# 64-dimension attention heads taken in pairs, one head on each half of TensorE's array

## The chip, the cores and the metric

One core of one Trainium2 chip runs the whole program. The metric is the device time of one execution in microseconds (us). The kernel before took 1958.06 us, the median of 3 runs (1953.44 to 1959.31).

The engines are named as in the profile: PE is TensorE's matmul side and PEld its weight loads, DVE is VectorE, ACT is ScalarE, POOL is GpSimd, SP is SyncE, which here only issues DMAs. SBUF is the on-chip memory, PSUM the eight accumulator banks that PE writes (128 partitions, 512 float32 columns in each bank).

## The reference, cut to what matters

Two two-layer models run one after the other over 256 tokens of width 1024, in float32. Four places in them are attention. Two have heads of 64 output dimensions:

```python
# layer 0 of the first model: 8 neighbourhood heads and 8 latent (MLA) heads
sc = einsum('bchd,bicjhd->bhcij', q_row, k_win) * 64 ** -0.5 + bias
p = softmax(sc);  out = einsum('bhcij,bicjhd->bchd', p, v_win)
# ...
q = concat([q_nope (64), rope(q_pe) (32)]);  k = concat([k_nope, k_pe])   # 96 wide
sc = einsum('bqhd,bkhd->bhqk', q, k) * 96 ** -0.5
p = softmax(sc);  out = einsum('bhqk,bkhd->bqhd', p, v)                   # v is 64 wide
# layer 1 of the first model: 16 dilated heads, 3 window groups each
sc = where(valid, einsum('bqhd,bqjhd->bhqj', q_blk[gi], k_sel[gi]) * 64 ** -0.5, NEG_INF)
outs, lses = softmax-weighted values and log-sum-exp of each group
out = sum(softmax(lses) * outs)
```

The other two (memory attention and forgetting attention in the second model) have heads of 128 dimensions. Around them stand norms and the large projections and MLPs, which make up most of the work.

## The kernel before, in words

The program is a list of stages made by `make_plan`; each engine walks the same list, and semaphores tie the engines together. Nothing is scheduled automatically: the order on each engine is the order in which the code is written. Between attention stages PE multiplies weight chunks that SP has loaded, ACT has rounded (`W_hi`, L914) and DVE has split (`W_lo`, L1127).

An attention stage (`kind == "attend"`) has a list of heads. The stage named "even" has 8 neighbourhood heads followed by 8 latent heads; "dilated" has 16 heads with three key groups; "memory0" has 4 and "fox" 12 heads of 128 dimensions. For each head n the engines do this:

- PE `scores(n)` (L680): queries times keys for two blocks of 128 queries. The stationary operand has 64 partitions for a neighbourhood or dilated head (partitions 0 to 63 for an even head, 64 to 127 for an odd one, `pb`), 96 for a latent head. One call in the code is two recorded matmuls, because the operands are plain float32. A neighbourhood or latent head has 4 recorded matmuls of 256 columns; a dilated head has 4 of 256 and 8 of 128.
- DVE `soft(n)`: scale and bias into SBUF (L1166 dilated, L1174 neighbourhood), then the row maximum (L1199). A latent head has only the maximum, read from PSUM (L1161, L1162).
- ACT `exps(n)` (L983): two exponentials with their row sums.
- DVE `normalise(n)`: reciprocal (L1204) and two multiplications (L1207).
- PE `transposes(n)` (L698): 4 transposes of the 128x128 blocks of probabilities, 8 for a dilated head.
- ACT `keep_pt(n)` (L993): the transposed probabilities from PSUM to SBUF, one copy of 512 columns, two for a dilated head.
- PE `values(n)` (L712, for the other two groups of a dilated head L719): values (stationary, 64 columns wide) times probabilities. The output lands on PSUM partitions 0 to 63 or 64 to 127 of bank 2 or 3.
- DVE `output(n)` (L1218): that result to SBUF.

PE's order per head is `transposes(n)`, `scores(n+3)`, `values(n)`. DVE's is `normalise(n+1)`, `output(n-1)`, `soft(n+3)`; ACT's is `keep_pt(n)`, `exps(n+2)`. The first heads' scores are issued inside the last projection of the stage before (`open_attention`): 3 heads for "even", 2 for "dilated". DVE runs their `soft` there too, ahead of the copy that ends the projection (L1345, L1364). Two heads before the end ACT also stages the input of the projection that follows (`stage_early`, L976), whose first matmul is L600.

## Time and profile before

| | |
|---|---|
| span of the profiled execution | 1952.7 us |
| its whole time | not recorded apart from the span; the 3 timed runs took 1953.44, 1958.06 and 1959.31 us |
| PE busy | 1882.7 us (96%) |
| DVE, ACT, POOL busy | 1219.9, 933.9, 273.2 us (62%, 48%, 14%) |
| mean granted TensorE clock | 0.992 |
| "even" attention, first transpose to the matmul behind it | 86.55 to 128.28 us |
| "dilated" attention, the same | 571.90 to 644.98 us |
| DMA busy share in the middle of both | 0.00 to 0.01 |

The page says that PE carries most of the chain that ended last. The two stages touched by the change are 42 and 73 us of the 1953. In a timeline row the first number is the start, the second the time from the first start to the last end of the merged instructions, so rows of pipelined matmuls overlap a little; in the chain the pieces add up.

### The profile page before, as it was taken

Reading aid. Unit: us, or ns where it says so; the run is one execution under the profiler, and the core shown is the slowest. Engines: PE = TensorE matmul, PEld = TensorE weight load, DVE = VectorE, ACT = ScalarE, POOL = GpSimd, SP = SyncE. Lnnn points to the kernel's source line nnn. Section 1 sums busy time; section 2 is a strip of 40 time slices with the busy share of each in tenths; the row PEclk is TensorE's granted clock in tenths of the full one; section 3 lists DMA queues with packets and bytes.
Section 4 is the critical chain, followed back from the end, with each engine's and each line's share of the span. In section 5 each row is a group of like instructions: output and inputs, shape, how many; then the busy total and the mean of one; then the engine's idle time right before and its main releaser. Section 6 shows DMA issues by size and latency. Waiting matters only on the chain.

```text
span 1952.7 us, 27728 instructions
## 1 busy us (share of the span) xinstructions
PE 1882.7 (96%) x9804; PEld 1580.0 (81%) x9804; DVE 1219.9 (62%) x1452; ACT 933.9 (48%) x1384; POOL 273.2 (14%) x219
## 2 busy tenths in 40 slices
PE   8899999999999999999999999999999999989998
PEld 6668887777778788888888878888888888778886
DVE  6866645766778566465656656664646656756654
ACT  5354444334345544454445445454544545545453
POOL 2110012211200101220011750002000011020012
PEclk9899999999999999999999999999999999999999
DMA  5415555454430465545555535555535555345553
GB/s 189 172 49 167 174 195 190 154 176 166 156 125 1 126 187 192 192 160 191 190 183 183 193 131 179 186 178 196 186 110 192 193 175 191 108 140 162 182 191 131
DMA packets 214812, 319.32 MB, mean 164 GB/s; under 512 B 5984, under 2 KB 167008, under 8 KB 214496
## 3 DMA queue, kind: packets, MB, share of 16 engines
q1 hardware_dynamic: 213616, 313.45, 48.6%
q0 software_dynamic: 848, 4.85, 0.6%
q8 instruction: 37, 0.61, 0.1%
q10 hardware_dynamic: 288, 0.23, 0.0%
q14 instruction: 23, 0.19, 0.0%
HBM read 317.46 MB, written 1.05 MB: 163 GB/s over the span
## 4 chain that ended last, share of the span: by engine, by line
PE 87%; DVE 9%; ACT 2%; issue 2%; POOL 1%; DMA 0%; DVEq 0%; ACTq 0%; POOLq 0%
PE PS L595 24%; PE PS L600 12%; PE PS L602 12%; PE PS L601 12%; PE PS L593 12%; DVE W_lo L1127 4%; PE PS L589 4%; PE PS L680 3%; PE PS L712 2%; PE PS L590 2%; PE PS L698 1%; PE PS L665 1%; PE PS L719 1%; DVE U L1374 1%; DVE U L1375 0%
## 5 line engine op out<-in xcount | busy, mean ns | idle before, releaser
L1127 DVE TENSOR_TENSOR W_lo<-W_raw,W_hi 128x1024 fp32r<-128x1024 f32 x598 | 772.7, 1333 | 290.7 <-ACT W_hi L914 289.4
L595 PE MATMUL PS<-XN,W_hi 128*128 128x512 f32 x2072 | 739.3, 396 | 0.0
L914 ACT ACTIVATE W_hi<-W_raw 128x1024 fp32r<-128x1024 f32 x598 | 598.3, 1050 | 183.0 <-PE PS L602 172.0
L593 PE MATMUL PS<-XN,W_lo 128*128 128x256 f32 x2072 | 578.9, 279 | 0.0
L595 PEld LDWEIGHTS PS<-XN,W_hi 128*128 128x128 f32 x2072 | 389.2, 188 | 79.9
L593 PEld LDWEIGHTS PS<-XN,W_lo 128*128 128x128 f32 x2072 | 391.1, 189 | 13.9
L1536 POOL TENSOR_TENSOR SX<-U,SX 128x512 fp32r<-128x512 f32 (+1 forms) x98 | 128.8, 1319 | 1352.2 <-ACT SX L976 1352.2
L600 PE MATMUL PS<-W_hi,SX 128*128 128x512 f32 x780 | 303.9, 390 | 1.4 <-issue 1.3
L601 PE MATMUL PS<-W_lo,SX 128*128 128x512 f32 x780 | 303.1, 389 | 0.0
L602 PE MATMUL PS<-W_hi,SX 128*128 128x512 f32 x780 | 303.0, 389 | 0.0
L927 ACT ACTIVATE T<-PS 128x512 f32<-128x512 f32 x152 | 91.0, 599 | 437.7 <-PE PS L595 437.7
L1138 DVE TENSOR_TENSOR T<-PS,T 128x512 f32<-128x512 f32 x128 | 88.5, 691 | 244.1 <-ACT T L927 244.1
L600 PEld LDWEIGHTS PS<-W_hi,SX 128*128 128x128 f32 x780 | 146.4, 188 | 32.4 <-issue 2.5
L602 PEld LDWEIGHTS PS<-W_hi,SX 128*128 128x128 f32 x780 | 146.4, 188 | 30.5
L976 ACT ACTIVATE SX<-U 128x512 fp32r (+2 forms) x98 | 60.6, 629 | 230.5 <-PE PS L602 230.5
L601 PEld LDWEIGHTS PS<-W_lo,SX 128*128 128x128 f32 x780 | 146.4, 188 | 30.1
L600 PE MATMUL PS<-W_hi,XN 128*128 128x512 f32 (+2 forms) x368 | 144.3, 392 | 15.0 <-DVE W_lo L1127 13.2
L601 PE MATMUL PS<-W_lo,XN 128*128 128x512 f32 (+2 forms) x368 | 141.7, 385 | 0.0
L602 PE MATMUL PS<-W_hi,XN 128*128 128x512 f32 (+2 forms) x368 | 141.6, 385 | 0.0
L589 PE MATMUL PS<-XN,W_hi 128*128 128x512 f32 x296 | 119.0, 402 | 8.6 <-DVE W_lo L1127 7.6
L600 PEld LDWEIGHTS PS<-W_hi,XN 128*128 128x128 f32 x368 | 70.2, 191 | 33.4 <-DVE W_lo L1127 19.6
L590 PE MATMUL PS<-XN,W_lo 128*128 128x256 f32 x296 | 82.4, 278 | 0.0
(145 smaller groups left out, 1599.3 us busy)
## 6 DMA issues: line engine op xcount, KB each, us to landing
W_raw<-in_ffn_w_gate_up SPq DMA_DIRECT2D x88, 1024.0 KB, 5.1
W_raw<-in_mlp_w SPq DMA_DIRECT2D x64, 1024.0 KB, 5.2
W_raw<-in_ffn_w_down SPq DMA_DIRECT2D x44, 1024.0 KB, 4.9
W_raw<-in_od_w_in SPq DMA_DIRECT2D x36, 1024.0 KB, 5.2
W_raw<-in_a_w_in SPq DMA_DIRECT2D x14, 1024.0 KB, 5.0
W_raw<-in_mem_w_kv SPq DMA_DIRECT2D x8, 1024.0 KB, 5.3
W_raw<-in_w_kvf SPq DMA_DIRECT2D x8, 1024.0 KB, 5.4
W_raw<-in_ev_w_in SPq DMA_DIRECT2D x6, 1024.0 KB, 5.3
```

The lines of the kernel that those rows point to most:

```text
L589: mm(bank, wT(W_hi, slot, k, fb), both, start=True, stop=False)
L590: mm(bank[:, S:], wT(W_lo, slot, k, fb), xn[:, k, 0, :], start=False, stop=False)
L593: mm(bank[:, S:], wT(W_lo, slot, k, fb), xn[:, k, 0, :], start=False, stop=False)
L595: last = mm(bank, wT(W_hi, slot, k, fb), both, start=False, stop=k == KD - 1)
L600: mm(bank, xh, wh, start=start, stop=False)
L601: mm(bank, xh, wl, start=False, stop=False)
L602: return mm(bank, xl, wh, start=False, stop=stop)
L914: A(W_hi[:, slot, halves(h)], W_raw[:, slot, halves(h)], ACT.Copy).then_inc(w_hi, 1)
L927: A(T0[:, pair, :].rearrange("p (f t) -> p f t", f=2), PS[:, 2 * pair:2 * pair + 2, S:2 * S], ACT.Copy).then_inc(cross_out, 1)
L1127: V.tensor_tensor(W_lo[:, slot, halves(h)], W_raw[:, slot, halves(h)], W_hi[:, slot, halves(h)], ALU.subtract).then_inc(w_lo, 1)
L1138: return V.tensor_tensor(dst.rearrange("p (f t) -> p f t", f=2), PS[:, 2 * pair:2 * pair + 2, 0:S], T0[:, pair, :].rearrange("p (f t) -> p ...
L1536: nc.gpsimd.tensor_tensor(SX[:, slot, 1, 0:st["ks"] * S], down_src(st, j), SX[:, slot, 0, 0:st["ks"] * S], ALU.subtract).then_inc(st_lo, 1)
```

## The change

In the stages "even" and "dilated" heads are taken in units of two (an even head and the odd head after it); in "memory0" and "fox" a unit is one head, and the order there stays as it was.

- `scores(u)` issues the two heads' calls alternately. For neighbourhood and dilated heads one is on array rows 0 to 63, the other on rows 64 to 127, each with its own PSUM banks. Latent heads have 96 rows each.
- `values(u)` issues the two heads' calls alternately, one on columns 0 to 63 and one on columns 64 to 127, into the two partition halves of one bank, and counts once on its semaphore.
- `output(u)` copies both halves with one instruction of 128 partitions.
- Transposes, exponentials, maxima and normalisations keep their number and size, but stand in twos.
- The look-ahead is in units. "Even": scores and `soft` lead by 2 units, with 2 units' scores issued in the opening. "Dilated": by 1 unit, with single-buffered score banks; probabilities alternate between two places, the transposed ones have one place.

The line numbers of the new kernel differ: L680 became L707, L698 L725, L712 L742, L719 L751; on DVE L1166 became L1211, L1199 L1244, L1204 L1249, L1207 L1252, L1218 L1264; on ACT L983 became L1022, L993 L1032.

```diff
-                 sm=18752, pt=19776, mem=20800, kpe=22848)
+                 sm=18752, pt=20800, mem=20800, kpe=22848)
...
+                st["paired"] = st["name"] in ("even", "dilated")
+                st["size"] = 2 if st["paired"] else 1
+                st["u0"] = len(units)
+                st["units"] = range(len(units), len(units) + len(st["what"]) // st["size"])
+                units += [range(len(heads) + i, len(heads) + i + st["size"])
+                          for i in range(0, len(st["what"]), st["size"])]
...
-            e["score_banks"] = (4 + n % 2 * 2, 5 + n % 2 * 2) if e["G"] == 3 else (4 + n % 3,)
+            u, i = e["unit"], e["slot"]
+            e["score_banks"] = ((4 + 2 * i, 5 + 2 * i) if e["G"] == 3 else
+                                (4 + 2 * (u % 2) + i,) if e["paired"] else (4 + n % 3,))
...
+            if e["G"] == 3:
+                e["probs"] = region(at + i * width, width) if u % 2 == 0 else T[:, i * width:(i + 1) * width]
+                e["ptile"] = [region(e["R"]["pt"] + (2 * i + g) * 512, 512) for g in range(2)]
+                e["pt_free"] = u
+            elif e["paired"]:
+                e["probs"] = region(at + (2 * (u % 2) + i) * width, width)
+                e["ptile"] = [region(e["R"]["pt"] + (2 * (u % 2) + i) * 512, 512)]
+                e["pt_free"] = u - 1
+            else:
+                e["probs"] = region(at + (n % 3) * width, width) if n % 3 < 2 else T1
+                e["ptile"] = [region(e["R"]["pt"] + (n % 2) * 512, 512)]
+                e["pt_free"] = u - 1
+
+            back = n - 2 * 2 if e["paired"] else n - 3
+            e["probs_back"] = back if back >= 0 and heads[back]["paired"] == e["paired"] else None
...
-        opened = lambda st: 3 if st["name"] in ("even", "fox") else 2
+        opened = lambda st: {"even": 2, "dilated": 1, "memory0": 2, "fox": 3}[st["name"]]
...
-            def scores(n):
-                e = heads[n]
-                for prev in e["score_prev"]:
-                    if heads[prev]["bias"]:
-                        pe.wait_ge(s_read, heads[prev]["read"] + 1)
-                    else:
-                        pe.wait_ge(s_exp, 2 * prev + 2)
+            def scores(u):
+
+                both = [heads[n] for n in units[u]]
+                for e in both:
+                    for prev in e["score_prev"]:
+                        if heads[prev]["bias"]:
+                            pe.wait_ge(s_read, heads[prev]["read"] + 1)
+                        else:
+                            pe.wait_ge(s_exp, 2 * prev + 2)
                 for t in range(TT):
-                    for g in range(e["G"]):
-                        at = e["cols"][t].start + (S + (g - 1) * P if g else 0)
-                        keys = (slice(t * P, (t + 1) * P) if g else
-                                slice(0, min(S, e["cols"][t].stop - at)))
-                        last = mm(e["scores"][:, at:at + keys.stop - keys.start],
-                                  e["q"][g][:, t * P:(t + 1) * P], e["k"][g][:, keys],
-                                  start=True, stop=True)
+                    for g in range(both[0]["G"]):
+                        for e in both:
+                            at = e["cols"][t].start + (S + (g - 1) * P if g else 0)
+                            keys = (slice(t * P, (t + 1) * P) if g else
+                                    slice(0, min(S, e["cols"][t].stop - at)))
+                            last = mm(e["scores"][:, at:at + keys.stop - keys.start],
+                                      e["q"][g][:, t * P:(t + 1) * P], e["k"][g][:, keys],
+                                      start=True, stop=True)
                 last.then_inc(s_score, 1)
...
-            def values(n):
-                e = heads[n]
-                if n >= 2:
-                    pe.wait_ge(h_done, e_out_done(n - 2))
-                d = 64 if e["pb"] or e["bias"] in ("na", "dil") or e["scale"] == 96 ** -0.5 else P
-                o = PS[e["pb"]:e["pb"] + d, 2 + n % 2, 0:S]
-                pe.wait_ge(s_pte, e["group0"] + 1)
+            def values(u):
+
+                both = [heads[n] for n in units[u]]
+                if u >= 2:
+                    pe.wait_ge(h_done, e_out_done(units[u - 2][-1]))
+                for e in both:
+                    d = (64 if e["paired"] else P)
+                    e["o"] = PS[e["pb"]:e["pb"] + d, 2 + u % 2, 0:S]
+                pe.wait_ge(s_pte, both[-1]["group0"] + 1)
                 for kt in range(TT):
-                    skip = P if kt and e["bias"] == "fox" else 0
-                    last = mm(o[:, skip:], e["v"](0, kt), e["ptile"][0][:, kt * S + skip:(kt + 1) * S],
-                              start=kt == 0, stop=kt == TT - 1 and e["parts"] == 1)
-                if e["parts"] == 2:
-                    pe.wait_ge(s_pte, e["group0"] + 2)
+                    for e in both:
+                        skip = P if kt and e["bias"] == "fox" else 0
+                        last = mm(e["o"][:, skip:], e["v"](0, kt),
+                                  e["ptile"][0][:, kt * S + skip:(kt + 1) * S],
+                                  start=kt == 0, stop=kt == TT - 1 and e["parts"] == 1)
+                if both[0]["parts"] == 2:
+                    pe.wait_ge(s_pte, both[-1]["group0"] + 2)
                     for g in (1, 2):
                         for t in range(TT):
-                            at = (g - 1) * S + t * P
-                            last = mm(o[:, t * P:(t + 1) * P], e["v"](g, t),
-                                      e["ptile"][1][:, at:at + P], start=False,
-                                      stop=g == 2 and t == TT - 1)
+                            for e in both:
+                                at = (g - 1) * S + t * P
+                                last = mm(e["o"][:, t * P:(t + 1) * P], e["v"](g, t),
+                                          e["ptile"][1][:, at:at + P], start=False,
+                                          stop=g == 2 and t == TT - 1)
                 last.then_inc(s_pv, 1)
...
-                    for n_ in range(opened(st), 3):
-                        scores(a0 + n_)
-                    for n_ in range(a0, a0 + m):
-                        transposes(n_)
-                        if n_ + 3 < a0 + m:
-                            scores(n_ + 3)
-                        values(n_)
+                    us = st["units"]
+                    if not st["paired"]:
+                        for u in us[opened(st):3]:
+                            scores(u)
+                    for u in us:
+                        if st["name"] == "dilated" and u + 1 in us:
+                            scores(u + 1)
+                        for n_ in units[u]:
+                            transposes(n_)
+                        if st["name"] == "even" and u + 2 in us:
+                            scores(u + 2)
+                        if not st["paired"] and u + 3 in us:
+                            scores(u + 3)
+                        values(u)
...
-                    if n > 1:
-                        act.wait_ge(s_pv, n - 1)
+                    if e["pt_free"] > 0:
+                        act.wait_ge(s_pv, e["pt_free"])
...
+                    if st["name"] == "even":
+                        exps(a0 + 2)
+                        exps(a0 + 3)
+                    lead = 2 if st["name"] in ("memory0", "fox", "even") else 1
+                    for u in st["units"]:
+                        for n_ in units[u]:
+                            keep_pt(n_)
+                        if u + lead in st["units"]:
+                            for n_ in units[u + lead]:
+                                exps(n_)
+                        if u == st["units"][-1] - (2 if st["size"] == 1 else 1):
...
-            def output(n):
-                e = heads[n]
-                dve.wait_ge(s_pv, n + 1)
-                d = e["y"].shape[0]
-                y, o = e["y"], PS[e["pb"]:e["pb"] + d, 2 + n % 2, 0:S]
+            def output(u):
+
+                e = heads[units[u][0]]
+                dve.wait_ge(s_pv, u + 1)
+                o = PS[:, 2 + u % 2, 0:S]
+                y = region(e["y_at"], S)
                 if e["bias"] == "dil":
                     y = y.rearrange("p (j r) -> p r j", r=RES)
                     o = o.rearrange("p (r j) -> p r j", r=RES)
-                V.tensor_copy(y, o).then_inc(h_done, 1)
+                V.tensor_copy(y, o).then_inc(h_done, len(units[u]))
...
-                    normalise(a0)
-                    soft(a0 + 2)
-                    for n_ in range(a0, a0 + m):
-                        if n_ + 1 < a0 + m:
-                            normalise(n_ + 1)
-                        if n_ > a0:
-                            output(n_ - 1)
-                        if n_ + 3 < a0 + m:
-                            soft(n_ + 3)
-                    output(a0 + m - 1)
+                    us = st["units"]
+                    if st["name"] == "dilated":
+                        for u in us:
+                            for n_ in units[u]:
+                                normalise(n_)
+                            if u > us[0]:
+                                output(u - 1)
+                            if u + 1 in us:
+                                for n_ in units[u + 1]:
+                                    soft(n_)
+                        output(us[-1])
+                        continue
+                    first = 2 if st["paired"] else 3
+                    done = st["size"] * (1 if st["paired"] else 2)
+                    if not st["paired"]:
+                        normalise(a0)
+                    for n_ in range(a0 + done, a0 + st["size"] * first):
+                        soft(n_)
+                    if st["paired"]:
+                        for n_ in units[us[0]]:
+                            normalise(n_)
+                    for u in us:
+                        if u + 1 in us:
+                            for n_ in units[u + 1]:
+                                normalise(n_)
+                        if u > us[0]:
+                            output(u - 1)
+                        if u + first in us:
+                            for n_ in units[u + first]:
+                                soft(n_)
+                    output(us[-1])
```

PE in the middle of the dilated stage, before, one head (`U`, `T` are SBUF, `PS` PSUM, `K` constants with the identity):

```order
L698 MATMUL PS<-K,U 128x128 x8
L680 MATMUL PS<-U 128x256
L680 MATMUL PS<-U 128x128 x2
L680 MATMUL PS<-U 128x256
L680 MATMUL PS<-U 128x128 x2
L712 MATMUL PS<-U 64x256 x2
L719 MATMUL PS<-U 64x128 x4
```

and now, one unit of two heads (the alternating calls of the two heads read as one row of double count):

```order
L725 MATMUL PS<-K,U 128x128 x16
L742 MATMUL PS<-U 64x256 x4
L751 MATMUL PS<-U 64x128 x8
L707 MATMUL PS<-U 128x256 x2
L707 MATMUL PS<-U 128x128 x4
L707 MATMUL PS<-U 128x256 x2
L707 MATMUL PS<-U 128x128 x4
L725 MATMUL PS<-K,T 128x128 x16
```

Twelve score calls, sixteen transposes and twelve value calls now stand together, where half of each stood before.

DVE in the same place, before, one head:

```order
L1166 SCALAR_TENSOR_TENSOR U<-PS,K 128x1024 [waits s_pt,s_score]
L1199 TENSOR_REDUCE ST<-U 128x2 [waits s_read]
L1204 RECIPROCAL ST<-ST 128x2 [waits s_exp]
L1207 TENSOR_SCALAR U<-U,ST 128x512 [waits dve_chain]
L1207 TENSOR_SCALAR U<-U,ST 128x512
L1218 COPY U<-PS 64x4x64 [waits s_pv]
```

and now, one unit:

```order
L1249 RECIPROCAL ST<-ST 128x2 [waits s_exp]
L1252 TENSOR_SCALAR T<-T,ST 128x512 [waits dve_chain]
L1252 TENSOR_SCALAR T<-T,ST 128x512
L1249 RECIPROCAL ST<-ST 128x2 [waits s_exp]
L1252 TENSOR_SCALAR T<-T,ST 128x512 [waits dve_chain]
L1252 TENSOR_SCALAR T<-T,ST 128x512
L1264 COPY U<-PS 128x4x64 [waits s_pv]
L1211 SCALAR_TENSOR_TENSOR U<-PS,K 128x1024 [waits s_pt,s_score]
L1244 TENSOR_REDUCE ST<-U 128x2 [waits s_read]
L1211 SCALAR_TENSOR_TENSOR U<-PS,K 128x1024 [waits s_pt,s_score]
L1244 TENSOR_REDUCE ST<-U 128x2 [waits s_read]
```

The reciprocals, which wait for the exponentials, now follow directly the `soft` (L1211, L1244) whose result those exponentials read; before, one other head's `soft` and one other head's normalisation lay in between.

ACT among the latent heads of the stage "even", before:

```order
L993 ACTIVATE U<-PS 128x512 [waits s_pv,s_pt]
L983 ACTIVATE T,ST<-PS,ST 128x256 [waits s_soft]
L983 ACTIVATE T,ST<-PS,ST 128x256
L993 ACTIVATE U<-PS 128x512 [waits s_pv,s_pt]
L983 ACTIVATE U,ST<-PS,ST 128x256 [waits s_soft]
```

and now:

```order
L1032 ACTIVATE U<-PS 128x512 [waits s_pv,s_pt] x2
L1022 ACTIVATE U,ST<-PS,ST 128x256 [waits s_soft]
L1022 ACTIVATE U,ST<-PS,ST 128x256
L1022 ACTIVATE U,ST<-PS,ST 128x256 [waits s_soft]
L1022 ACTIVATE U,ST<-PS,ST 128x256
L1032 ACTIVATE U<-PS 128x512 [waits s_pv,s_pt] x2
```

The two copies of transposed probabilities (L1032) of a unit stand behind the four exponentials of the unit after it.

## Rows read from the trace of the kernel before

**Rows 1.** The page, part 4: the chain that ended last, by engine.

```profile
PE 87%; DVE 9%; ACT 2%; issue 2%; POOL 1%; DMA 0%; DVEq 0%; ACTq 0%; POOLq 0%
```

**Rows 2.** Stretch of ten heads: us, PE, PEld, DVE, ACT, POOL busy; clock, DMA, GB/s.

```profile
572.92:621.46 48.54, 48.54 (x322) 39.62 (x321) 40.96 (x63) 24.98 (x61) 0.00 (x0) 1.00 0.00 1
```

**Rows 3.** Chain through one head of that stage: start us, us, what.

```profile
576.82 1.03 PE PS L698 x8
...
577.84 1.95 PE PS L680 x12
...
579.79 1.01 PE PS L712 x4
...
580.80 0.87 PE PS L719 x8
```

**Rows 4.** Timeline there: start us, us, engine, line, operation, tiles, shapes, count.

```profile
584.68 1.23 DVE L1166 SCALAR_TENSOR_TENSOR U<-PS,K 128x1024 f32<-128x1024 f32 x1 [0.71 <-PE PS L680]
...
585.94 1.22 DVE L1199 TENSOR_REDUCE ST<-U 128x2 f32<-128x1024 f32 x1
...
587.08 0.15 DVE L1204 RECIPROCAL ST<-ST 128x2 f32<-128x2 f32 x1
...
587.15 1.09 ACT L993 ACTIVATE U<-PS 128x512 f32<-128x512 f32 x2 [2.37 <-PE PS L698]
...
588.06 0.62 DVE L1218 COPY U<-PS 64x256 f32<-64x256 f32 x1
```

**Rows 5.** Timeline at that stage's end: one head's exponentials on ACT.

```profile
636.65 0.72 ACT L983 ACTIVATE U<-U,ST 128x512 f32<-128x512 f32 x1
...
637.97 0.20 ACT L983 ACTIVATION_READ_ACCUMULATOR U<-U,ST 128x1 f32 x1
```

**Rows 6.** Timeline, PE: score matmuls of three heads, of one, of two.

```profile
79.50 1.99 PE L680 MATMUL PS<-U 64*128 64x256 f32 x12
...
96.62 1.13 PE L680 MATMUL PS<-U 64*128 64x256 f32 x4
...
559.53 3.44 PE L680 MATMUL PS<-U 64*128 64x256 f32 x24
```

**Rows 7.** Timeline, DVE, one neighbourhood head.

```profile
95.17 0.76 DVE L1174 SCALAR_TENSOR_TENSOR T<-PS,U 128x256 f32<-128x256 f32 x2
...
96.56 0.15 DVE L1204 RECIPROCAL ST<-ST 128x2 f32<-128x2 f32 x1
...
97.78 0.76 DVE L1174 SCALAR_TENSOR_TENSOR U<-PS,U 128x256 f32<-128x256 f32 x2
```

**Rows 8.** Timeline, DVE and ACT, latent heads.

```profile
115.19 0.69 DVE L1161 TENSOR_REDUCE ST<-PS 128x2 f32<-128x512 f32 x1 [0.39 <-PE PS L680]
...
115.99 0.16 DVE L1204 RECIPROCAL ST<-ST 128x2 f32<-128x2 f32 x1
...
119.74 0.47 ACT L983 ACTIVATE T<-PS,ST 128x256 f32<-128x256 f32 x1
...
120.55 0.21 ACT L983 ACTIVATION_READ_ACCUMULATOR T<-PS,ST 128x1 f32 x1
```

**Rows 9.** Chain: score matmuls of two latent heads, one after the other.

```profile
106.91 0.87 PE PS L680 x4
...
109.37 0.87 PE PS L680 x4
```

**Rows 10.** Timeline, PE: the first transposes of the first attention stage.

```profile
86.55 0.63 PE L698 MATMUL PS<-K,U 128*128 128x128 f32 x4 [2.13 <-DVE U L1207]
```

**Rows 11.** The three microseconds after them, columns as in rows 2.

```profile
88.20:91.50 3.30, 3.30 (x10) 1.82 (x10) 2.68 (x9) 0.99 (x5) 0.00 (x0) 0.50 0.00 0
```

**Rows 12.** Timeline: first matmul behind each stage, copy ahead of the second's.

```profile
128.28 0.50 PE L600 MATMUL PS<-W_hi,SX 128*128 128x512 f32 x1
...
644.98 0.50 PE L600 MATMUL PS<-W_hi,SX 128*128 128x512 f32 x1
...
568.67 1.23 DVE L1364 COPY U<-PS 128x1024 f32<-128x1024 f32 x1 [0.72 <-PE PS L602]
```

More of the change, by code:

```diff
@@ L360, in head @@
             v = lambda g, kt: region(RB[f"mem_v{l}"] + kt * 512 + h * P, P)
[L361 to L364 removed]
+            y = H0 + (8 + h) * S
+            return dict(G=1, q=[q], k=[k], v=v, y_at=y, pb=0, scale=P ** -0.5, bias=None, R=RB, h=h)
+        heads, units, n_groups = [], [], 0
         h_count = 0
@@ L373, in build_program @@
                     e["group0"] = n_groups
+                    e["unit"] = next(u for u in st["units"] if len(heads) in units[u])
+                    e["slot"] = len(heads) - units[e["unit"]][0]
+                    e["paired"] = st["paired"]
                     e["parts"] = 2 if e["G"] == 3 else 1
@@ L411, in build_program @@
                 last_score[b] = n
-            e["pt_banks"] = [0, 1] if e["G"] == 3 else [n % 2]
+            e["pt_banks"] = [0, 1] if e["G"] == 3 else [i if e["paired"] else n % 2]
             e["pt_prev"] = []
@@ L419, in build_program @@
             width = e["w"] * TT
-            e["probs"] = (region(e["R"]["sm"] + (n % 3) * width, width) if n % 3 < 2
-                          else T[:, 0:width] if e["G"] == 3 else T1)
             e["read"] = n_read
             n_read += bool(e["bias"])
-            e["ptile"] = [region(e["R"]["pt"] + ((n % 2) * e["parts"] + g) * 512, 512)
-                          for g in range(e["parts"])]
-            e["mx"] = ST[:, 8 + 8 * (n % 3):10 + 8 * (n % 3)]
-            e["z"] = ST[:, 10 + 8 * (n % 3):12 + 8 * (n % 3)]
-            e["rz"] = ST[:, 12 + 8 * (n % 3):14 + 8 * (n % 3)]
+            at = e["R"]["sm"]
+            if e["G"] == 3:
[12 more added lines that the diff above has]
+            e["probs_back"] = back if back >= 0 and heads[back]["paired"] == e["paired"] else None
+            if e["probs_back"] is None and n >= 4:
+                e["probs_back"] = n - 3
+            r = 8 + 8 * (n % 4 if e["paired"] else n % 3)
+            e["mx"], e["z"], e["rz"] = ST[:, r:r + 2], ST[:, r + 2:r + 4], ST[:, r + 4:r + 6]
         k_norm = k_turn = n_glu = n_staged = n_cross = 0
@@ L730, in open_attention @@
                     pe.wait_ge(mla_a, 2)
-                for n in range(opened(st)):
-                    scores(st["a0"] + n)
+                for u in st["units"][:opened(st)]:
+                    scores(u)
             def turn_memory():
@@ L1153, in soft @@
                 e = heads[n]
-                dve.wait_ge(s_score, n + 1)
-                if n >= 3:
-                    back = heads[n - 3]
+                dve.wait_ge(s_score, e["unit"] + 1)
+                if e["probs_back"] is not None:
+                    back = heads[e["probs_back"]]
                     dve.wait_ge(s_pt, back["group0"] + back["parts"])
```

25 lines of the change are left out of this document (9 added, 16 removed).

## The prediction, made before the changed kernel was run

> **What bounds the kernel now.** I read the chain that ended last first: PE carries 87% of it, DVE 9% [rows 1]. So inside an attention stage I looked for the engine that the others wait for. In the dilated stage, over ten heads (48.54 us), PE is busy throughout, DVE 40.96 us, ACT 24.98 us, clock 1.00, no DMA [rows 2]. The chain shows one head as four pieces of PE: transposes 1.03, scores 1.95, values 1.01 and 0.87, together 4.85 us [rows 3]. DVE's `soft` waits there for scores (0.71 us idle, [rows 4]). PE bounds this stage, with DVE close behind. Among the neighbourhood heads of "even" DVE starts a `soft` every 2.61 us (95.17 to 97.78) [rows 7] and is all but full; the latent heads come every 2.46 us (106.91 to 109.37) [rows 9] and DVE waits 0.39 us in each for scores [rows 8]: PE bounds them. All else in the program keeps its order on every engine, so the sum is over these two stages.
>
> **Do matmuls on the two row halves overlap?** Before, heads of opposite halves stood next to each other only in the openings. One head's 4 score matmuls span 1.13 us [rows 6] and add 0.85 to 0.87 us each time more follow on the same array. Three heads in a row, halves 0, 1, 0, span 1.99 us where serial work would need 1.13 + 2 x 0.85 = 2.8; that is two heads' work (1.13 + 0.85 = 1.98), so the middle head was free. Two dilated heads span 3.44 us, not 2 x 1.95 = 3.9 [rows 3, 6]: they overlapped only where one ended. So rows overlap in plain float32.
>
> No row shows two column halves side by side. Bounds for a pair's value matmuls: fully parallel, one head's 1.88 us (1.01 + 0.87, [rows 3]); serial 3.76. Below nothing makes no sense, as the streaming is the same; above serial neither. I take parallel with one matmul of skew, 2.1 us, because the row halves do it. The Trainium skill ("TensorE: Matmul & The Clock Gate", Part 3) gives 2.38 times for three column tiles, which no run here shows; by it a pair would come to some 2.4 us by estimate. The same section says that a weight load overlaps running matmuls only when the row group differs; that would speak for the serial case, which is the first rival.
>
> **The dilated stage, pair by pair.** PE needs per pair: scores one head's 1.95 plus 0.2 skew = 2.15, values 2.1, transposes 2 x 1.03. The second head's transposes use the first one's PSUM banks, so they start about 1.3 us after the first one's (half of its transposes 0.52 [rows 3], one copy of 0.54, half of ACT's 1.09 [rows 4], and a hop each way, some 0.2). Values wait a like time: 2.7 + 2.1 + 2.15 = 7.0 us.
>
> DVE per head: `soft` 2.40 us (584.68 to 587.08), normalisation 0.98 (to 588.06), output 0.65 [rows 4]. A pair needs 2 x 2.40 + 2 x 0.98 + one output = 7.4 us. But normalising a unit now follows its own `soft` at once, while before another head's work lay between. Call t0 the time when DVE has issued the second `soft`. Its maximum ends 0.08 us later (585.94 + 1.22 against 587.08); the exponentials take 1.52 us (636.65 to 637.97 + 0.20, [rows 5]); with semaphore hops the second reciprocal starts at t0 + 1.67. The first normalisation covers 0.98 of it: 0.69 us of new idle. The cycle is 1.67 + 0.98 + 0.65 + 4.80 = 8.1 us per pair, against 9.70 before. DVE, not PE, is the bound (8.1 against 7.0), so the gain is 1.6 us a pair, not 2.7. Behind DVE's waiting reciprocal stand the output and the next unit's `soft`; PE's next transposes wait for them, and nothing else hides it.
>
> Start: the 24 score matmuls in the opening take 2.15 instead of 3.44 us, but DVE then does the two `soft` before the copy, and the copy's idle is 0.72 us [rows 12]: it comes 0.7 us earlier, at 568.0. The next unit's scores run 569.2 to 571.35, its two `soft` to t0 = 576.2. Six cycles: t0 of the last unit 576.2 + 48.6 = 624.8. End: second normalisation done t0 + 2.7, transposes from t0 + 3.5 (ACT's staging for the next projection is ahead of the copies), value matmuls from 4.9 to 7.0, the next projection at t0 + 7.2 = 632.0. Before it was 644.98 [rows 12]. That is 13 us; I take off 1 for hops that I rounded down: **12 us**.
>
> **The stage "even".** Neighbourhood pair: DVE `soft` 1.39 us (95.17 to 96.56), normalisation with output 1.22 (to 97.78) [rows 7], exponentials about 1.1 us as for latent heads (119.74 to 120.76, [rows 8], plus 0.09). Cycle 1.23 + 1.22 + 2.78 = 5.23 us, against 5.22: nothing gained; the second output saved is spent on the wait for exponentials. Latent pair: the 96 rows do not fit two halves, so scores cost 2 x 0.87 [rows 9]. PE: transposes 1.03 (eight, [rows 3]), scores 1.74, values 1.25: 4.0 us. DVE: 1.2 + 1.22 + 2 x 0.80 [rows 8] = 4.0. There is also a loop through ACT, which copies a unit's transposed probabilities only after the next unit's exponentials: 1.15 + copies 1.09 + hop 0.14 + values 1.25 + transposes 1.03 + scores 1.74 + hop 0.1 + two `soft` 1.6 = 8.1 over two cycles. I take 4.15 us against 4.92.
>
> Opening: two more `soft` (2.8 us) precede the first normalisation, so the first transposes start at about 89.4 instead of 86.55. Before, PE idled 2.13 us there [rows 10] and its granted clock was then 0.50, that is 1.2 GHz, in the next stretch [rows 11]; now it idles some 5 us and will drop as well. At 1.2 GHz transposes, scores and hops bring the third unit's scores to 93.9, t0 of unit 2 is 96.7, unit 3 101.95, unit 4 106.0, the last 106.0 + 3 x 4.15 = 118.4; the end as above, t0 + 7.2 = 125.6 against 128.28 [rows 12]: 2.7 us. I take off 0.7 for a longer time at 1.2 GHz: **2 us**.
>
> **Sum.** 14 us off the span: 1952.7 to 1938.7. The median of the runs lies 5.4 us above the span; with that kept, 1958.1 - 14 = **1944 us**.
>
> **Rivals.**
> 1. Column halves do not overlap. PE per dilated pair 2.7 + 3.9 + 2.15 = 8.8 us: above DVE's 8.1, still under 9.70. Six cycles cost 4.2, the last values 1.8: 6.5 us gained there. Latent pairs come to 4.9, the gain of "even" is nil. 1952 us. For it: no row shows the overlap. Against: the row halves have it. 0.16.
> 2. DVE's hops are longer than I read them (the new idle 1.3 instead of 0.69 us a pair, both stages): 8.7 us a pair, 5 us less gained, 1949 us. For it: my hops are read from waits that were not tight. 0.08.
> 3. Slower: PE now idles in every dilated pair, about 1 us of 8.1, and between the two heads' transposes, and the granted clock falls to 1.2 GHz as it did behind 2.13 us of idle [rows 10, 11]. At that level the 6 us of streaming per pair take 12, with hops 12.6 against 9.70. From 3 pairs of 8 on the gain of this stage is gone; with all of them 23 us are lost and the time is 1979 us, with five of them 1966. Against: the new idle is two or three gaps of under 1 us in a pair, not 2.13 us in one. 0.07.
> 4. The change does not do what it says: alternating calls run in order even on rows, because one call is two recorded matmuls. Then a dilated pair is 2.7 + 3.9 + 3.9 = 10.5 us on PE, 0.8 more than before, and the kernel takes 1963 us. [Rows 6] speak against it. 0.03.
>
> **Chances.** Forecast 0.66 (1938 to 1949), the others 0.16, 0.08, 0.07, 0.03. A measurement of this kernel can tell 0.3%, 5.9 us, from no change. Faster by more than that: nearly all of the forecast, half of rival 1 and most of rival 2, 0.78. Within: 0.15. Slower: 0.07. The range reaches over rivals 1 and 2 and leaves the slower ones out: 1938 to 1956.
>
> **What would show it.** In the changed kernel's timeline: 24 dilated score matmuls of a unit in about 2.2 us and 24 value matmuls in about 2.1 (3.9 proves rival 1); DVE's dilated period 8.1 us per pair with one idle of about 0.7 us before the second L1249, released by ACT; PE waiting for DVE at the transposes; neighbourhood pairs still 5.2 us; latent pairs 4.15; the matmul behind the stages 2 us earlier for "even" and 14 us earlier for "dilated" (both stages). I am wrong if DVE's idle is larger, if the clock rows show 0.50 inside the stages beyond the opening, or if the later stages, whose order is the same, change length.

## The result, and the profile after

| | before | after |
|---|---|---|
| median | 1958.68 us | 1934.92 us |
| lowest and highest of 4 runs | 1953.44, 1959.89 | 1934.72, 1936.47 |
| span of the profiled execution | 1952.7 us | 1934.7 us |
| mean granted clock in it | 0.992 | 0.987 |
| PE busy | 1882.7 us | 1848.3 us |
| DVE busy | 1219.9 us | 1209.9 us |

The ratio is 0.9888, with a 95% interval from 0.9872 to 0.9905. By that ratio the kernel is some 22 us faster; the two medians of this table lie 23.8 us apart. The forecast was 1944 us with a range from 1938 to 1956: the sign was right, but the time came out 9 us below the forecast and lies outside the range.

The page's row of the chain, which answers to [rows 1]:

```profile
PE 82%; DVE 11%; issue 3%; ACT 2%; DMA 1%; POOL 1%; DVEq 0%; ACTq 0%; POOLq 0%
```

PE carries less, DVE more. The busy time by stretch (us, PE, PEld, DVE, ACT, POOL busy; clock, DMA, GB/s), for the middle of "even" and for most of the dilated stage, to be read beside [rows 2]:

```profile
94.00:117.00 23.00, 19.85 (x132) 14.23 (x128) 19.99 (x62) 16.15 (x55) 0.00 (x0) 1.00 0.00 1
571.44:620.17 48.73, 37.30 (x388) 31.17 (x387) 44.03 (x69) 32.60 (x77) 0.00 (x0) 0.99 0.01 2
```

Before, PE was busy throughout such a stretch. Now it is busy 37.3 of 48.7 us, and DVE 44.0: the bound has changed hands. One dilated pair on PE, from the timeline:

```profile
578.24 2.03 PE L707 MATMUL PS<-U 64*128 64x256 f32 x24
580.28 1.09 PE L725 MATMUL PS<-K,U 128*128 128x128 f32 x8
581.96 1.09 PE L725 MATMUL PS<-K,U 128*128 128x128 f32 x8 [0.59 <-DVE U L1252]
583.39 1.08 PE L742 MATMUL PS<-U 128*64 128x256 f32 x8 [0.34 <-ACT U L1032]
584.28 1.07 PE L751 MATMUL PS<-U 128*64 128x128 f32 x16
586.14 2.03 PE L707 MATMUL PS<-U 64*128 64x256 f32 x24 [0.79 <-DVE T L1211]
```

The reader is to see two things. The 24 score matmuls of two heads take 2.03 us; the 12 of one head took 1.95 in the chain before [rows 3], and two dilated heads in a row took 3.44 [rows 6]. The value matmuls of two heads, 8 and 16, take 1.08 and 1.07 us; those of one head, 4 and 8, took 1.01 and 0.87 in the chain [rows 3]. Both kinds overlap all but fully. And PE now waits in three places of a pair: 0.59 us for the second head's normalisation, 0.34 for ACT's copy, 0.79 for DVE's reading of the scores.

DVE over the same pair, which answers to [rows 4]:

```profile
579.15 0.15 DVE L1249 RECIPROCAL ST<-ST 128x2 f32<-128x2 f32 x1
...
580.82 0.17 DVE L1249 RECIPROCAL ST<-ST 128x2 f32<-128x2 f32 x1 [0.60 <-ACT U L1022]
581.02 0.88 DVE L1252 TENSOR_SCALAR U<-U,ST 128x512 f32<-128x512 f32 x2
581.82 0.62 DVE L1264 COPY U<-PS 128x256 f32<-128x256 f32 x1
582.26 1.23 DVE L1211 SCALAR_TENSOR_TENSOR T<-PS,K 128x1024 f32<-128x1024 f32 x1
...
587.05 0.15 DVE L1249 RECIPROCAL ST<-ST 128x2 f32<-128x2 f32 x1
```

The period is 587.05 - 579.15 = 7.90 us, with one idle of 0.60 us, for the second head's exponentials.

Two rows from the openings and ends, of PE. The first is the first transposes of "even", after 4.90 us of idle where [rows 10] show 2.13. The others are the first matmul behind each stage, which [rows 12] show at 128.28 and 644.98:

```profile
88.93 1.94 PE L725 MATMUL PS<-K,U 128*128 128x128 f32 x8 [4.90 <-DVE U L1252]
...
122.85 0.50 PE L624 MATMUL PS<-W_hi,SX 128*128 128x512 f32 x1
...
626.91 0.50 PE L624 MATMUL PS<-W_hi,SX 128*128 128x512 f32 x1
```

So "even" ends 5.4 us earlier and the dilated stage 18.1, that is 12.6 more by these two rows. Behind it the two traces keep that distance to the end, to within 0.5 us: 18.0 us of span.

### The profile page after: what moved, and what is told of

The parts are those of the page before. It is cut to its first block, busy times and chain, and to the rows that moved or that the text cites. A ratio compares the mean times of both kernels' runs of the same rounds, so it can differ in the third digit from the quotient of the medians.

```text
span 1934.7 us, 27716 instructions
## 1 busy us (share of the span) xinstructions
PE 1848.3 (96%) x9804; PEld 1558.3 (81%) x9804; DVE 1209.9 (63%) x1436; ACT 935.0 (48%) x1384; POOL 271.9 (14%) x219
## 3 DMA queue, kind: packets, MB, share of 16 engines
q1 hardware_dynamic: 213616, 313.45, 48.7%
## 4 chain that ended last, share of the span: by engine, by line
PE 82%; DVE 11%; issue 3%; ACT 2%; DMA 1%; POOL 1%; DVEq 0%; ACTq 0%; POOLq 0%
PE PS L619 24%; PE PS L617 12%; PE PS L624 12%; PE PS L626 12%; PE PS L625 12%; DVE W_lo L1172 5%; PE PS L613 4%; PE PS L614 2%; PE PS L707 1%; PE PS L689 1%; PE PS L725 1%; DMA W_raw<-in_mem_w_kv 1%; DVE U L1420 1%; PE PS L742 1%; ACT U L1022 0%
```

## The experiments

Ratios are to the kernel before on the same chip. Line numbers are those of the changed kernel unless said.

### How much does a single run tell?

**The changed kernel again**, unchanged, 5 rounds. Expected:

> The changed kernel once more, as the yardstick for the others. If the 23.8 us between the medians are all the kernel's, it comes to 1935 us again, within 2, and the kernel before stays at 1958 to 1960. Rival: 18 us are the kernel's, as between the two profiled spans (1952.7 and 1934.7), and the rest is that the kernel before varies from run to run; then among the new runs of the kernel before some stand near 1953.

Measured: 1936.29 us (1935.10 to 1937.21), ratio 0.9893 (0.9874 to 0.9913). The kernel before ran 11 times beside it, from 1950.8 to 1962.4 us. So each answer holds for one kernel: the changed one came back within 2 us of 1935, and four of the 11 runs of the kernel before stand between 1953.3 and 1954.3 us. The kernel before varies by over 11 us from run to run, the changed one by 2 here. In every run the time is the span plus 1.8 us, so nothing outside the span varies. The 11 runs of before order themselves by their mean granted clock: 1950.8 us at 0.995, 1953.4 and 1953.5 at 0.993, 1957.5 at 0.990, 1962.4 at 0.987.

**The kernel before again**, for a second trace. Expected:

> The kernel before, unchanged, for a second trace of it. Its runs lie between 1950.8 and 1962.4 us, with mean granted clocks from 0.995 to 0.987, and its profiled execution (1954.5) is one of the faster. Theory (the spread is the number of stretches of 3.4 us at clock 0.50, and nothing else): against the first trace the instructions on TensorE shift only where such a stretch stands in one trace and not in the other, each by 1 to 2 us. Rival (DMA or the start): the shift is where no such stretch is.

Measured: 1957.13 us, span 1955.3, clock 0.990. Aligned instruction by instruction, its PE is 0.6 us ahead of the first trace at 572 us, 2.7 us behind at 578, and nowhere else moves by more than 0.6 us at once; at the end it is 2.6 us behind. The same stretch, at the start of the dilated heads, in the first trace and in this one, each with the scores ahead of it (columns as above):

```profile
569.95 2.02 PE L680 MATMUL PS<-U 64*128 64x256 f32 x12 [1.32 <-DVE U L1364]
...
571.80:578.60 6.80, 6.80 (x47) 5.59 (x46) 6.46 (x10) 3.76 (x9) 0.00 (x0) 1.00 0.01 2
```

```profile
569.38 2.02 PE L680 MATMUL PS<-U 64*128 64x256 f32 x12 [1.31 <-DVE U L1364]
...
571.80:578.60 6.80, 6.80 (x24) 5.08 (x23) 4.97 (x7) 2.71 (x6) 0.00 (x0) 0.50 0.00 0
```

The granted clock is 1.00 in one and 0.50 in the other, so 2.4 and 1.2 GHz, with the same instructions in the same order behind the same 1.3 us of idle on PE (1.32 and 1.31). In 6.8 us PE did 47 matmuls in the one and 24 in the other. It costs 3.2 us, more than the 1 to 2 us that I had expected of a stretch of 3.4 us; this one is 6.8 us long. In these two traces the difference is this one stretch; of the other runs only the mean clock is on record, and it orders them the same way. The profiled execution of the kernel before had none there and was one of its faster ones: by the 1.8 us it took some 1954.5 us, 3.6 less than the median of 1958.06 us from which the forecast was made.

This trace and that of the changed kernel again were taken at nearly the same mean granted clock, 0.990 and 0.991. Their spans are 1955.3 and 1933.3 us, so 22.0 us apart, where the first two traces (0.992 and 0.987) are 18.0 apart. Aligned by instruction, 4.8 of the 22.0 have come by the end of "even", 16.0 more by the end of the dilated stage, and 1.2 from stretches of lower clock elsewhere.

### Is it the alternation?

**Value matmuls head by head**, the scores still alternating:

```diff
-                for kt in range(TT):
-                    for e in both:
+                for e in both:
+                    for kt in range(TT):
...
-                    for g in (1, 2):
-                        for t in range(TT):
-                            for e in both:
+                    for e in both:
+                        for g in (1, 2):
+                            for t in range(TT):
```

> The two heads' value matmuls one head after the other, scores still alternating, all else the same. If the column halves overlapping is worth something although VectorE bounds the dilated pairs: a pair's value matmuls take 3.7 us instead of 1.9, TensorE's loop in a dilated pair becomes about 2.7 + 3.7 + 1.95 = 8.35 us against VectorE's 7.9, a latent pair about 4.7 against 3.95, the ends 1.8 and 0.9 longer: 8 us in all, 1943 us. Rival: VectorE hides it, under 2 us more.

Measured: 1934.21 us (1932.65 to 1944.93), ratio 0.9890 (0.9865 to 0.9914): no loss. The first theory fell, the rival's answer came out, but not only for its reason. The timeline shows what the order did to PE:

```profile
583.12 1.09 PE L742 MATMUL PS<-U 128*64 128x256 f32 x8 [0.34 <-ACT U L1032]
584.00 1.53 PE L751 MATMUL PS<-U 128*64 128x128 f32 x16
585.78 2.02 PE L707 MATMUL PS<-U 64*128 64x256 f32 x24 [0.25 <-DVE T L1211]
```

The 8 of L742 take 1.09 us although they come head by head, the 16 of L751 take 1.53 instead of 1.07. The wait behind them shrank from 0.79 to 0.25 us (0.33 in the next pair), so it takes up what is lost, and DVE's period stays 7.90 us. The single records of those two groups, start and duration as the trace has them:

```
L742  583.115 0.401   583.128 0.430   583.352 0.379   583.395 0.379   583.568 0.379 ...
L751  584.000 0.273   584.109 0.272   584.218 0.273   584.327 0.272   584.436 0.273
      584.442 0.323   584.545 0.272   584.602 0.273 ...
```

Alone, a head's records of L751 start every 0.109 us; where more start, two heads run. By that step the eight of the first head are those from 584.000 to 584.764, and the second head's first one starts at 584.442, four steps in. (The records do not name their head; the steps alone tell them apart.) In L742 a head has only four, and two start together from the first on. That suggested, without showing it, that PE goes on past a matmul that has to wait for its half of the array, but only some records far. The Trainium skill ("TensorE: Matmul & The Clock Gate", Part 3) says that matmuls start and end in strict program order. By it a head's records would all stand ahead of the next head's, and the 16 would start over 15 steps; they start over 11.5 (584.000 to 585.257). These rows do not fit the rule.

**Score matmuls head by head**, the values still alternating (the same edit in `scores`):

> The two heads' score matmuls one head after the other, values still alternating. 24 score matmuls of a dilated unit then take 3.44 us as before instead of 2.0. Loop of TensorE in a dilated pair 2.7 + 1.9 + 3.44 = 8.0 us, about VectorE's 7.9: 1 us over eight pairs, and under 1 us in the openings: 1937 us. Rival: row alternation is the larger part of the gain (1.45 us a pair, 12 us in all): 1947 us.

Measured: 1937.97 us (1934.94 to 1940.56), ratio 0.9898 (0.9878 to 0.9919), within 1 us of what was expected. A pair's 24 scores take 3.44 us, and PE becomes the bound again at 8.10 us a pair, with no wait for DVE:

```profile
579.80 3.44 PE L707 MATMUL PS<-U 64*128 64x256 f32 x24
583.17 1.09 PE L725 MATMUL PS<-K,U 128*128 128x128 f32 x8
...
587.90 3.44 PE L707 MATMUL PS<-U 64*128 64x256 f32 x24
```

**Both head by head**:

> Neither alternates: pairs in the code's order and the merged output copy alone. If the overlap in the array is what pays, TensorE's loop in a dilated pair is 2.7 + 3.7 + 3.44 = 9.85 us (9.70 before), a latent pair 4.7 to 4.9: 1953 to 1957 us, about the kernel before. Rival: the new order and the halved number of switches between kinds of matmul pay: 1945 us or less.

Measured: 1940.63 us (1940.32 to 1941.35), ratio 0.9915 (0.9896 to 0.9934). A pair takes 8.55 us between the first transposes of two units:

```profile
575.72 1.09 PE L725 MATMUL PS<-K,T 128*128 128x128 f32 x8
...
578.56 1.09 PE L742 MATMUL PS<-U 128*64 128x256 f32 x8 [0.34 <-ACT U L1032]
579.44 1.53 PE L751 MATMUL PS<-U 128*64 128x128 f32 x16
580.90 3.44 PE L707 MATMUL PS<-U 64*128 64x256 f32 x24
584.27 1.09 PE L725 MATMUL PS<-K,U 128*128 128x128 f32 x8
```

The first theory fell again: with no alternation at all, some 17 of the 21 us by which the medians of this set differ are still there. The rival won on the number. But it names the wrong cause, as the next run shows.

**No neighbours on opposite halves.** In the dilated stage the two heads' value and score matmuls are issued in turn, `values(u, i)` and `scores(u, i)` being those of one head; only the first two units' scores still come as pairs:

```diff
...
-                        values(u)
+                        if st["name"] == "dilated" and u + 2 in us:
+                            for i in range(2):
+                                values(u, i)
+                                scores(u + 2, i)
+                        else:
+                            values(u)
...
```

> The changed kernel with one edit in the dilated stage: the value matmuls of a pair's first head, the score matmuls of the first head of the unit after the next, then the same two for the second heads. So no two heads' matmuls on opposite halves stand next to each other; units, merged output and buffers stay. The kernel with both alternations undone had still 2.34 us for a pair's values and 3.37 for its scores, since heads on opposite halves stand next to each other there too. Theory (the gain of the dilated stage is overlap of neighbours on opposite halves, in whatever order of calls): values 2 x 1.88, scores 2 x 1.95, transposes 2.84, so 10.5 us a pair against 7.90 in the changed kernel and 9.70 in the kernel before; six or seven cycles make the stage 16 to 18 us longer, the time is 1951 to 1954 us. Rival (the gain is in the merged output copy and the shorter wait for buffers): at most 9.0 us a pair, under 1945 us.

Measured: 1948.92 us (1945.93 to 1951.22), ratio 0.9957 (0.9940 to 0.9975). One unit of it on PE (L709 is the scores, L728 the transposes, L747 and L756 the values):

```profile
576.72 1.09 PE L728 MATMUL PS<-K,T 128*128 128x128 f32 x8
578.15 1.06 PE L728 MATMUL PS<-K,T 128*128 128x128 f32 x8 [0.34 <-ACT U L1043]
579.15 1.08 PE L747 MATMUL PS<-U 128*64 128x256 f32 x4
580.06 1.04 PE L756 MATMUL PS<-U 128*64 128x128 f32 x8
581.03 2.02 PE L709 MATMUL PS<-U 64*128 64x256 f32 x12
582.98 1.08 PE L747 MATMUL PS<-U 128*64 128x256 f32 x4
583.89 1.04 PE L756 MATMUL PS<-U 128*64 128x128 f32 x8
584.86 2.02 PE L709 MATMUL PS<-U 64*128 64x256 f32 x12
586.81 1.09 PE L728 MATMUL PS<-K,U 128*128 128x128 f32 x8
```

A unit takes 586.81 - 576.72 = 10.09 us, against 9.70 before the change. I had expected 10.5 and 1951 to 1954 us: the first value matmuls wait here for one head's copies only, which I had counted for both. Everything else of the change is still there, the merged copy among it, and the dilated stage has lost its gain: by the trace, aligned with the kernel before, it is 0.9 us slower (6.8 us of it ran at a granted clock of 0.50, none in that trace of the kernel before, so at like clock it may be a little faster), while "even", not touched by this edit, keeps 6.1 of its own.

The edit also brings back the changes between value and score matmuls that pairing had halved, which the rival of the run before had named. The rows speak against these: from the first value matmul to the first score matmul it is 1.88 us (579.15 to 581.03) and from there to the next value matmul 1.95 (581.03 to 582.98), just what one head's pieces took in the chain before [rows 3]; and 8 records of L742 of two heads span 1.09 us in the run before, as long as the 4 of one head here. So the dilated stage lives by overlap, and overlap needs only that the two heads stand next to each other. For "even" no run takes the neighbours apart; what makes its gain is read from rows only.

**Alternating by two calls** (four records of one head, then four of the other):

> The changed kernel, but its score and value matmuls alternate by two calls (four recorded matmuls) of one head instead of by one. With all calls of a head in a row, the second head's first matmul stood beside the first head's after four recorded matmuls (values L751: 584.442 against 584.000, the first four at 0.109 us steps), so the pair took 1.53 us instead of 1.07; four records per head (L742) took 1.08 in both orders. Theory (the array's queue reaches four recorded matmuls past one that waits for its half): 24 dilated scores in 2.03 to 2.2 us and 16 values in 1.07 to 1.1, as with strict alternation; time 1934 to 1937 us. Rival (each switch of halves costs, or only strict alternation overlaps fully): scores 2.5 us or more, values 1.3 or more.

Measured, one run: 1935.76 us. On PE:

```profile
583.07 1.09 PE L743 MATMUL PS<-U 128*64 128x256 f32 x8 [0.34 <-ACT U L1033]
583.96 1.09 PE L752 MATMUL PS<-U 128*64 128x128 f32 x16
585.82 2.10 PE L708 MATMUL PS<-U 64*128 64x256 f32 x24 [0.76 <-DVE T L1212]
```

Scores 2.10 against 2.03, values 1.09 against 1.07, the period 7.90 as before. That fits the theory that PE reaches over four waiting records; groups of more than four that still have the other head's behind them were tried only as whole heads. Put together, for one dilated pair:

| order of the calls | values, us (8 and 16) | scores, us (24) | pair, us | median |
|---|---|---|---|---|
| before the change | two heads apart | two heads apart | 9.70 | 1958 |
| heads kept apart | 1.08 + 1.04, twice | 2.02, twice | 10.09 | 1948.9 |
| head by head | 1.09 + 1.53 | 3.44 | 8.55 | 1940.6 |
| scores head by head | 1.08 + 1.07 | 3.44 | 8.10 | 1938.0 |
| values head by head | 1.09 + 1.53 | 2.02 | 7.90 | 1934.2 |
| by twos (one run) | 1.09 + 1.09 | 2.10 | 7.90 | 1935.8 |
| one by one (the change) | 1.08 + 1.07 | 2.03 | 7.90 | 1934.9 |

The last three have the same period with different PE work, which is DVE's bound at work.

### Filling DVE's idle

**The output copy between the two normalisations**, in both stages:

```diff
...
-                            for n_ in units[u]:
-                                normalise(n_)
+                            normalise(units[u][0])
                             if u > us[0]:
                                 output(u - 1)
+                            normalise(units[u][1])
...
```

> The changed kernel with one edit: on VectorE the merged output copy of the previous pair stands between the two normalisations of a pair instead of behind both, in both stages. In the changed kernel VectorE idles 0.60 us per dilated pair before the second L1249, released by ScalarE, and its period is 7.90 us; 0.44 and 0.28 us per pair in "even". Theory (VectorE is the bound and this wait is inside its loop): the copy (0.46 us to the next instruction) fills the idle, the dilated period becomes 7.44 to 7.5 us, eight pairs give 3.2 us; "even" gives 0.4 x 3 plus 0.28 x 4 = 2.3 us at most; the median is 1930 to 1932 us. Rival (TensorE is the bound, at some 7.5 us a pair): the matmuls of the next scores wait instead, the period stays above 7.7 and the time is that of the changed kernel, 1934 to 1937 us.

Measured: 1932.58 us (1927.63 to 1936.28), ratio 0.9880 (0.9859 to 0.9901); I had expected 1930 to 1932. DVE:

```profile
583.66 0.15 DVE L1249 RECIPROCAL ST<-ST 128x2 f32<-128x2 f32 x1
583.85 0.88 DVE L1252 TENSOR_SCALAR T<-T,ST 128x512 f32<-128x512 f32 x2
584.65 0.63 DVE L1264 COPY U<-PS 128x256 f32<-128x256 f32 x1
585.33 0.17 DVE L1249 RECIPROCAL ST<-ST 128x2 f32<-128x2 f32 x1
...
591.10 0.15 DVE L1249 RECIPROCAL ST<-ST 128x2 f32<-128x2 f32 x1
```

The idle is gone and the period is 7.44 us, as expected, so DVE is the bound and the wait was inside its loop. PE's wait for the scores' banks fell to 0.33 us. Since single runs spread over 9 us, the pair was run once more.

**Changed kernel and this version side by side**:

> The changed kernel once more, beside the version with the output copy between the two normalisations, on the same chip: 1935 to 1936.5 us. Its traces so far hold a total of 38.6 to 50.7 us at a granted clock of 0.50; each stretch of 3.4 us more or less moves the time by 1 to 1.7 us, so single runs may lie between 1933 and 1938.

> The version with the output copy between the normalisations, beside the changed kernel on the same chip. Its dilated pair took 7.44 us against 7.90 and its trace, aligned by instruction, gained 4.2 us in the two stages at like clock (0.5 in the stage even, 3.7 in the dilated one), and 4.4 more in places where the two kernels are the same and only the stretches of lower clock differ. Theory: 4 us less than the changed kernel, 1931 to 1932.5 us. Rival: what its TensorE saves comes back as more stretches of lower clock, since its first runs spread from 1927.6 to 1936.3 us: 1934 us or more.

Measured: 1935.42 us (1932.53 to 1938.27), ratio 0.9886 (0.9864 to 0.9907), and 1931.74 us (1928.43 to 1935.31), ratio 0.9870 (0.9846 to 0.9895). The medians differ by 3.7 us here, and by 2.3 to 3.7 with the earlier run and the two earlier medians of the changed kernel. Six periods of the dilated stage at 0.46 us less give 2.8 us of it. The intervals of the two ratios overlap, so by the times alone it is likely, not shown; the 7.44 us are shown. The version beats the kernel before clearly, and is the best of all that ran.

## Why the prediction was wrong, step by step

**What bounded the kernel before, and the overlap.** Right. Rows overlap (2.03 us against my 2.15), columns too, and without the skew that I gave them: 0.88 + 1.07 = 1.95 us against 2.1. Rival 1, serial columns, is out: the 8 values of both heads take 1.08 us, and so do the 4 of one head in the kernel with heads kept apart. The weight-load rule that I quoted from the Trainium skill ("TensorE: Matmul & The Clock Gate", Part 3) as an argument for the serial case does not limit this one: both column halves use all 128 rows, their row group is the same, and they ran side by side. Its factor of 2.38 for three column tiles would have made a pair 2.4 us by estimate; measured were 1.95 us for two heads, where one took 1.88.

**The dilated stage.** Right in mechanism; that the size came out too was in part luck. DVE became the bound. I forecast 8.1 us a pair with 0.69 us of new idle released by ACT; it was 7.90 with 0.60. The 0.2 us between them are the output copy: 0.65 in the sum, 0.44 from its start to the next instruction (581.82 to 582.26). Its forecast end of 632.0 us corresponds to 626.9 + 5.4 (what "even" had gained) = 632.3. The 12 us were 12.6.

But the sum was made at full clock, and in the profiled execution 3.4 us at the stage's opening and 6.8 us at its end ran at a granted clock of 0.50. From the first L1249 of the last pair to the next projection I forecast 7.2 us; it was 8.26 (618.65 to 626.91). With the scores head by head, whose trace shows a clock of 1.00 over the whole stage, the same work took 6.59:

```profile
620.45 0.15 DVE L1249 RECIPROCAL ST<-ST 128x2 f32<-128x2 f32 x1
...
627.04 0.50 PE L624 MATMUL PS<-W_hi,SX 128*128 128x512 f32 x1
```

At the opening the second pair's first L1249 came at 571.51 us, and at 570.49 in the second trace, where the clock stayed at 1.00. So at full clock the stage would gain some 15 us by estimate (12.6 + 1.7 + 1.0): the forecast of 12 was too small, and the lower clock made up for it.

**The stage "even".** Right in sign, too small: 2 us forecast, 5.4 measured. Both `soft` of unit 2 were out at 95.70 us, not 96.7. The neighbourhood pair took 5.08 us (95.70 to 100.78), not 5.23; a latent pair 3.95 (109.01 to 112.96), not 4.15. The end came 122.85 - 116.91 = 5.9 us after the last `soft`, not 7.2: I had carried the dilated stage's tail over, whose transposes and values are longer. Of the 3.4 us that were missing, 1.0 are the opening, 0.5 the cycles, 1.3 the tail (rounded), and 0.7 what I had taken off for a longer time at 1.2 GHz. That drop did come (the first transposes take 1.94 us instead of 1.09), but it was in the sum already.

**The step that failed: the base, on top of a sum that was too small.** "The median of the runs lies 5.4 us above the span; with that kept". It was 1936.47 - 1934.7 = 1.8 us between a run's span and its own time, in this run and in all others, and the rest was the luck of one execution: the profile of the kernel before was 3.6 us faster than its median, with no stretch of lower clock at the start of the dilated stage, where its second trace has one of 6.8 us. The profile after was 1.5 us slower than its median. These 5.2 us, with 3.4 in "even" and 0.6 in the dilated stage, are the 9 by which the forecast was off. Either alone would have left the time inside the range (1938.8 or 1940.0 us); both pushed the same way, and the range, made from mechanisms alone, had no place for the first.

The traces at like clock say the same in another way: they are 22.0 us apart, and the sum has 14. It is short by 2.8 in "even", by 4.0 in the dilated stage, and by 1.2 elsewhere. Outside the opening of "even", no term of it priced a stretch of lower clock in either kernel. Such a stretch of 6.8 us cost 3.2 us in the kernel before, where PE is busy throughout, and 1.7 us (8.26 against 6.59) at the end of the changed stage, where PE waits anyway.

**The clock rival.** It forecast 1.2 GHz throughout the dilated pairs from their small idles. The clock row over these pairs is 0.99. The rival's case did not come, though PE idles some 1.7 us of each 7.90 in three pieces. In the two stages, stretches at 0.50 came where PE had idled longer in one piece: around 4.90 us in "even", behind 1.92 us at the dilated opening, and around 2.83 us at its end, where the last transposes ran at half speed. The last row shows that this is no rule: in the second trace of the same kernel the 24 scores behind the same 1.92 us, and all work from there to 619.5 us, ran at 1.00.

```profile
563.59 2.61 PE L707 MATMUL PS<-U 64*128 64x256 f32 x24 [1.92 <-DVE U L1410]
...
619.78 1.97 PE L725 MATMUL PS<-K,T 128*128 128x128 f32 x8 [2.83 <-DVE T L1252]
```

```profile
563.63 2.03 PE L707 MATMUL PS<-U 64*128 64x256 f32 x24 [1.92 <-DVE U L1410]
```

**What stays open.** By instruction the two profiled executions differ by 18.0 us, the medians by 19 to 24 us, depending on the set of runs. The two profiled executions are not alike in clock: that of the kernel before had a higher one (0.992) than its usual run (0.990), that of the changed kernel a lower one (0.987). All runs on record with a mean clock of 0.990 took 1957.0 to 1961.0 us before (five runs) and 1932.5 to 1937.2 after (five runs). So the gain of the medians does not need the changed kernel to spend less time at 1.2 GHz. Why a stretch comes in one execution and not in the next was not settled; they shifted between traces of one and the same kernel.

## What to carry to other kernels

When two heads use opposite halves of the array, put their matmuls next to each other; exact alternation matters little, groups of four recorded matmuls overlap as well, and other work between them that needs part of both halves ends it. Once PE is relieved, look at the next engine's loop for a wait that another of its instructions can fill, as the output copy did here. And when a forecast is put on a median, take a profiled execution's own time (span plus the fixed part) and ask how the clock rows of that one execution stand to the usual run: here that was worth 3.6 us before and 1.5 after, more together than one of the two terms of the sum. Better still, compare traces of both kernels at like clock: 22.0 us here, where the first pair showed 18.0.

## What the hardware showed that was not expected

- Head-by-head order still overlaps in the value matmuls: from the first record on where a head has four (L742, 1.09 us for both heads), from the fifth on where it has eight (L751, 1.53 us).
- Column halves run wholly in parallel in plain float32: 8 value matmuls of two heads in 1.08 us, 4 of one head in 1.08.
- The same kernel, with the same instructions behind the same 1.3 us of idle on PE, ran a stretch of 6.8 us at 2.4 GHz in one execution and at 1.2 GHz in another, at a cost of 3.2 us.
- In these traces a lower clock cost less where PE also waits: 6.8 us at 0.50 cost 1.7 us at the end of the changed stage.
